# Projection on raw x with the row norm applied afterwards, and work moved around the first projection of a two-block kernel

## The reference

```python
hn = rmsnorm(h, mix_norm_pre)              # x * rsqrt(mean(x*x) + EPS) * g
proj = hn @ w_in                           # (256, 2048) @ (2048, 3616)
z, xbc, dt_raw, u = jnp.split(proj, split_at, axis=-1)
xbc = jax.nn.silu(dwconv_centred(xbc, conv_w, conv_b))     # 5 taps along the rows
dt = jax.nn.softplus(dt_raw + dt_bias)
y = y_fwd + y_bwd + xs * d_skip            # two chunked SSD scans, 16 heads, chunks of 128
y = y * jax.nn.silu(z)
y = y * lax.rsqrt(jnp.mean(y * y, axis=-1) + EPS) * norm_w  # over 512 channels
y_pool = pool_mixer(u, pool_w, pool_scale)                 # mean windows 2, 4, 8, 16
mix = jnp.concatenate([y_ssd, y_pool], axis=-1) @ w_out
h = h + rmsnorm(mix, mix_norm_post)
```

## Time and profile before

| | us |
|---|---|
| median of 3 runs | 2986.96 (2986.94 to 2986.97) |
| the profiled execution, its own time | 2987.04 |
| its span in the trace | 2985.3 |
| PE busy | 2897.9 (97%) |
| DVE busy | 1975.4 (66%) |
| ACT busy | 1346.4 (45%) |
| POOL busy | 15.8 |
| mean granted TensorE clock | 0.986 of full |

### The profile page before, as it was taken

The page is one execution under the profiler, slowest core; times in us unless marked ns, Lnnn a source line. Parts: engine busy times, 40 slices in busy tenths (PEclk is TensorE's granted clock), DMA queues, the critical chain, the costliest instruction groups (busy, mean ns, idle before and its releaser), DMA issues.

```text
span 2985.3 us, 34913 instructions
## 1 busy us (share of the span) xinstructions
PE 2897.9 (97%) x13750; PEld 2394.7 (80%) x13750; DVE 1975.4 (66%) x2531; ACT 1346.4 (45%) x1657; POOL 15.8 (1%) x33
## 2 busy tenths in 40 slices
PE   6998999999999999999999999999989999999999
PEld 6987878888888887778888777778878888888887
DVE  3765789898986666852437777767766656655444
ACT  3444454444444445632324555554444444444333
POOL 1000000000000000000000000000000000000000
PEclk8999999999999999999999999999999999999999
DMA  5443768778778777623346655547766777776564
GB/s 177 142 121 106 222 194 255 246 241 251 253 254 256 246 246 247 223 78 93 93 120 189 176 177 179 181 130 241 236 196 205 219 222 218 221 214 209 191 191 154
DMA packets 301692, 583.25 MB, mean 195 GB/s; under 512 B 20699, under 2 KB 21177, under 8 KB 300889
## 3 DMA queue, kind: packets, MB, share of 16 engines
q1 hardware_dynamic: 299705, 573.57, 62.1%
q0 software_dynamic: 1824, 7.46, 0.8%
HBM read 578.85 MB, written 2.10 MB: 195 GB/s over the span
## 4 chain that ended last, share of the span: by engine, by line
PE 92%; DVE 4%; ACT 1%; issue 1%; DMA 0%; SPq 0%; ACTq 0%; DVEq 0%
PE psum L496 21%; PE psum L499 21%; PE psum L498 21%; PE psum L554 3%; PE psum L556 3%; PE psum L555 3%; PE psum L2547 2%; PE psum L2549 2%; PE psum L2548 2%; PE psum L469 2%; PE psum L471 2%; PE psum L472 2%; PE psum L2565 1%; PE psum L2575 1%; PE psum L515 1%
## 5 line engine op out<-in xcount | busy, mean ns | idle before, releaser
L674 DVE TENSOR_TENSOR w_lo<-w_raw,w_hi 128x1024 fp32r<-128x1024 f32 x720 | 877.6, 1224 | 592.6 <-ACT w_hi L609 588.9
L609 ACT ACTIVATE w_hi<-w_raw 128x1024 fp32r<-128x1024 f32 x720 | 762.8, 1060 | 1048.4 <-PE psum L499 1046.2
L496 PE MATMUL psum<-w_hi,x_split 128*128 128x512 f32 x1984 | 782.9, 395 | 8.6 <-issue 5.3
L499 PE MATMUL psum<-w_hi,x_split 128*128 128x512 f32 x1984 | 775.0, 391 | 0.0
L498 PE MATMUL psum<-w_lo,x_split 128*128 128x512 f32 x1984 | 774.5, 390 | 0.0
L496 PEld LDWEIGHTS psum<-w_hi,x_split 128*128 128x128 f32 x1984 | 373.9, 188 | 86.1 <-issue 8.0
L499 PEld LDWEIGHTS psum<-w_hi,x_split 128*128 128x128 f32 x1984 | 373.6, 188 | 78.7
L498 PEld LDWEIGHTS psum<-w_lo,x_split 128*128 128x128 f32 x1984 | 374.2, 189 | 75.1
L654 DVE TENSOR_TENSOR w_lo<-w_raw,w_hi 128x1024 fp32r<-128x1024 f32 x104 | 126.8, 1225 | 238.6 <-ACT w_hi L591 238.6
L496 PE MATMUL psum<-w_hi,hidden_split 128*128 128x512 f32 x704 | 274.8, 390 | 0.0
L630 DVE SCALAR_TENSOR_TENSOR stat<-w_raw,conditions,stat 128x512 f32<-128x512 f32 x360 | 269.8, 750 | 6.8
(11 more groups left out here) (324 smaller groups left out, 3470.5 us busy)
## 6 DMA issues: line engine op xcount, KB each, us to landing
w_raw<-in_w_in SPq DMA_DIRECT2D x216, 512.0 KB, 3.7
w_raw<-in_w_ada SPq DMA_DIRECT2D x192, 512.0 KB, 4.6
w_raw<-in_w_ffn_up SPq DMA_DIRECT2D x176, 512.0 KB, 4.6
w_raw<-in_w_ffn_down SPq DMA_DIRECT2D x88, 512.0 KB, 5.6
w_raw<-in_w_ff_gate SPq DMA_DIRECT2D x88, 512.0 KB, 3.9
w_raw<-in_w_ff_up SPq DMA_DIRECT2D x88, 512.0 KB, 4.4
w_raw<-in_w_ff_down SPq DMA_DIRECT2D x88, 512.0 KB, 4.4
w_raw<-in_w_out SPq DMA_DIRECT2D x64, 512.0 KB, 5.1
```

The source lines that it names most:

```text
L496: nc.tensor.matmul(to, x_hi[:, tokens], hi, start=u == 0 and t == 0, stop=False, skip_group_check=True)
L499: mm = nc.tensor.matmul(to, x_lo[:, tokens], hi, start=False, stop=end and t == 1, skip_group_check=True)
L609: nc.scalar.activation(w_hi[:, b.slot(n)], raw[:, b.raw_slot(k)], ACT.Copy).then_inc(w_rounded, 1)
L674: nc.vector.tensor_tensor(w_lo[:, slot], raw[:, b.raw_slot(k)], r(w_hi[:, slot]), ALU.subtract).then_inc(w_split, 1)
```

## The change

- x is no longer scaled before it is turned. PE turns raw x, ACT and DVE split x times gain at once (`hi_pair`, `lo_pair`). The sums of squares move into the stream (ACT, steps 0 to 2). `r_spread` spreads 1/rms over the partitions as a row `RROW`, and DVE multiplies each group's PSUM by it: in place for B, C and xs, into the buffers for u and z, where ACT copied before. ACT applies silu to z from the buffer.
- SP loads the identity, one gain, then for each quarter of the columns two pieces of x and a weight block; all other parameters and the dt weights are loaded by POOL. Their turning on PE is behind unit 3.
- The dt product is made of split values (48 fp32r matmuls), channels of dt on the partitions, behind unit 4; two transposes follow at step 6.
- The running sums of dt are held as hi and lo (`ROWS`, 64 rows, fp32r), and `rows` uses them with a selector `SEL` (fp32r).
- The taps of a group are done 8 in its last step and 8 in the step behind it. `cumulate` is at step 11 (before 13), `dt_done` at 9 (before 10), `pool_product` at 48, 49, 50, 52.
- `y_stat` makes two columns instead of a spread row (8 matmuls with one column), the root and the reciprocal are of 128x2, and `y_spread` spreads the result. The second half of y (y products 30 and 31, `y_out(7)`, `gate_y(1)`, norm and split) is beside out's first group, and out's units wait for the mix splits in five pieces.
- `PAIR_AT`, the spacing of the SSD pairs by two steps from the second on, is the same in both kernels.

The diff, cut to its core:

```diff
+            sp.dma_start(C[:, 0:P], consts_d[:, 0:P]).then_inc(S("start_landed"), 16)
+            sp.dma_start(*params[0]).then_inc(S("start_landed"), 16)
+            for k in range(4):
+                for c in range(2):
+                    sp.dma_start(H[:, c, columns_of(k)], A["x"][0, c * P:(c + 1) * P, columns_of(k)]
+                                 ).then_inc(S(f"x_landed{k}"), 16)
+                sp.dma_start(raw[:, k], source("in", PHASES["in"].body[k])).then_inc(w_landed[k], 16)
...
+                    if name == "in" and k < 4:
+                        continue
+                    if name == "in" and k == RAW + 2:
+                        sp.dma_start(C[:, P:], consts_d[:, P:]).then_inc(S("consts_landed"), 16)
...
+            for to, src in params[1:]:
...
+            pool.dma_start(WDT, W_IN[:, :, 2560:2592]).then_inc(S("wdt_landed"), 16)
...
+        IN_TURN = [-1, -1, -1, -1, 0, 0, 1, 1]
...
-        POOL_AT = [49, 50, 52, 53]
+        POOL_AT = [48, 49, 50, 52]
+        MIX = [(8, 10), (10, 12), (12, 16), (0, 4), (4, 8)]
...
+            act.wait_ge(S("mix_gain"), 1)
+            for k in range(4):
+                hi_pair(act, "mix_pre", 2 * k, XS, lambda t: prm("mix_pre", t))
+                hi_pair(act, "mix_pre", 2 * k + 1, XS, lambda t: prm("mix_pre", t))
+                first_hi(k)
...
+            def x_square(c):
+                for k in range(4):
+                    act.wait_ge(S(f"x_landed{k}"), 32)
+                square_part(act, "mix_pre", H[:, c, :], c, 0, SQ0)
...
-                group_used(act, b, k)
                 if j < 3:
                     t0 = X_TILE[j]
+                    act.wait_ge(S("in_scaled"), j + 1)
                     first_tap(act, lambda f: accf(b.set(j), f), lambda f: XBC[:, t0 + f],
...
+            def z_silu(g):
+                act.wait_ge(evacuated, 2 + 6 + g)
+                nc.scalar.activation(SZ[:, 4 * g:4 * g + 4], SZ[:, 4 * g:4 * g + 4], ACT.Silu
+                                     ).then_inc(S("z_ready"), 1)
...
-                nc.scalar.activation(ST[0:32, :], PS[0:32, 6, :], ACT.Copy).then_inc(S("acum_rows"), 1)
+                nc.scalar.activation(ROWS[0:64], PS[0:64, 6, :], ACT.Copy).then_inc(S("acum_hi"), 1)
...
+            def in_early(n):
+                if n == IN_END - 1:
+                    group_used(act, PHASES["in"], n)
+                    mix_hi(0)
...
-                [(PRE_SPLIT[i], lambda k: kept_hi(act, "mix_pre", k, XS), i) for i in range(4, 8)] +
-                [(2, conditions, None), (5, dt_exp, None), (8, dt_ln, None), (14, acum_rows, None)] +
+                [(0, x_square, 0), (1, x_square, 1), (2, lambda _: std_act(act, "mix_pre"), None)] +
+                [(5, conditions, None), (7, dt_exp, None), (9, dt_ln, None), (12, acum_rows, None)] +
...
                 [(at + 1, pool_out, g) for g, at in enumerate(POOL_AT)] +
-                [(52, y_square, 0), (56, mix_hi, 2), (56, mix_hi, 3), (57, y_root, 0), (58, y_square, 1),
-                 (59, mix_hi, 0), (60, y_root, 1), (61, mix_hi, 1)], "in", IN_END)
-            stream_act(act, "in", in_evac, late)
+                [(49, y_square, 0), (54, y_root, 0), (56, mix_hi, 1), (56, mix_hi, 2), (57, mix_hi, 3), (57, z_silu, 1)],
...
+            for k in range(4):
+                lo_pair(dve, "mix_pre", 2 * k, XS, lambda t: prm("mix_pre", t))
+                lo_pair(dve, "mix_pre", 2 * k + 1, XS, lambda t: prm("mix_pre", t))
+                first_lo(k)
...
+            def skip_rows(_):
+                all_params(dve)
...
+            def params_copy(_):
+                dve.wait_ge(S("params_pe"), 1)
...
+            def dt_scale(_):
+                dve.wait_ge(S("dt_by_heads"), 1)
+                ch.wait()
+                nc.vector.tensor_tensor(ST[0:32, 0:L], PS[0:32, 4, 0:L], RROW[0:32], ALU.mult).then_inc(S("dt_scaled"), 1)
...
-                for j in others:
+                for j in others if only is None else only:
...
+                    nc.vector.tensor_tensor(acc(b.set(j)), acc(b.set(j)), over_tiles, ALU.mult
+                                            ).then_inc(S("in_scaled"), 1)
+                    dve.wait_ge(S("in_scaled"), j + 1)
+                    conv_half(j, 0)
...
+                    t = slice(4 * (j - 3), 4 * (j - 3) + 4)
+                    dve.wait_ge(S("u_padded"), 1)
+                    nc.vector.tensor_tensor(UP[:, t, 8:8 + L], acc(b.set(j)), over_tiles, ALU.mult).then_inc(evacuated, 1)
...
+                    z_scale(0)
...
+            def conv_half(j, half):
+
+                b, t0 = PHASES["in"], X_TILE[j]
+                conv(lambda f: accf(b.set(j), f), lambda f: XBC[:, t0 + f], 5,
+                     lambda tap, f: prm("ssd_conv_w", 12 * tap + t0 + f), lambda f: 4 * j + f + 1, evacuated,
+                     (0, 1) if half == 0 else (3, 4))
...
+                for s in range(2):
+                    nc.vector.scalar_tensor_tensor(DA[:, :, s], c32(dtv), -1.0, over_chunks(SM[:, 64:96]),
+                                                   ALU.mult, ALU.mult).then_inc(S("da_ready"), 1)
...
-                [(at, next_split, 4 + 2 * at) for at in range(2)] +
-                [(1, lambda_sums, None), (3, minus_lambda, None), (4, dt_bias, None), (6, dt_plus_one, None),
-                 (10, dt_done, None), (13, masked_cb, 0),
-                 (14, masked_cb, 1), (14, acum_columns, None)] +
+                [(8 * j + 8, lambda j: conv_half(j, 1), j) for j in range(3)] +
+                [(2, skip_rows, None), (3, params_copy, None), (3, lambda _: rstd_dve(dve, "mix_pre"), None),
+                 (3, wdt_lo, None), (4, rstd_row, None), (5, dt_scale, None), (5, lambda_sums, None), (6, dt_bias, None),
+                 (6, minus_lambda, None), (8, dt_plus_one, None), (9, dt_done, None), (12, acum_columns, None),
+                 (12, acum_lo, None), (13, masked_cb, 0), (14, masked_cb, 1)] +
...
-                [(STEP_AT[4 * t + 3] + 6, y_out, t) for t in range(8)] +
+                [(STEP_AT[4 * t + 3] + 6, y_out, t) for t in range(7)] +
...
-                [(51, gate_y, 0), (57, mix_lo, (0, 2)), (58, gate_y, 1), (58, mix_lo, (1, 3)), (59, y_recip, 0),
-                 (59, y_norm, 0), (60, mix_lo, (2, 0)), (61, y_recip, 1), (61, y_norm, 1), (62, mix_lo, (3, 1))],
...
+                [(48, gate_y, 0), (54, y_recip, 0), (56, mix_lo, 1), (56, y_norm, 0), (56, z_scale, 1), (56, mix_lo, 2),
+                 (57, mix_lo, 3)], "in", IN_END)
+            stream_dve(dve, "in", in_evac, late, early=lambda n: mix_lo(0) if n == IN_END - 1 else None)
...
+            def out_late(j, u):
+                if (j, u) == (0, 0):
+                    y_out(7)
+                    gate_y(1)
+                if (j, u) == (0, 2):
+                    y_recip(1)
+                if (j, u) == (0, 3):
+                    y_norm(1)
+                if (j, u) == (0, 4):
+                    mix_lo(4)
+
...
+            def r_spread(_):
+                k = RMS.index("mix_pre")
+                pe.wait_ge(rms_rstd, rms_count("mix_pre"))
+                pe.wait_ge(pre_ready, pre_count("mix_pre", 8))
+                for c in range(2):
+                    mm = nc.tensor.matmul(PS[:, 7, c * P:c * P + P], RS[:, k, c:c + 1].to_broadcast([P, P]), ident,
+                                          start=c == 0, stop=True, skip_group_check=True)
+                mm.then_inc(S("r_spread"), 1)
...
-                pe.wait_ge(pre_z, z_count("mix_pre", 8))
+                pe.wait_ge(S("wdt_split"), 1)
+                for t in range(KT):
+                    nc.tensor.matmul(PS[0:32, 4, 0:L], WDT_HI[:, t], XS[:, t, 0], start=t == 0, stop=False,
+                                     skip_group_check=True)
+                    nc.tensor.matmul(PS[0:32, 4, 0:L], WDT_HI[:, t], XS[:, t, 1], start=False, stop=False,
+                                     skip_group_check=True)
+                    mm = nc.tensor.matmul(PS[0:32, 4, 0:L], WDT_LO[:, t], XS[:, t, 0], start=False, stop=t == KT - 1,
...
-                pe.wait_ge(S("da_ready"), 1)
+                da = SM[:, 128:256].rearrange("p (c s h) -> p c s h", c=2, s=2)
...
+                    mm = nc.tensor.matmul(PS[:, 4 + m % 2, d * L:d * L + L], SEL[0:64, h:h + 1].to_broadcast([64, P]),
+                                          ROWS[0:64, d * L:d * L + L], start=d == 0, stop=True, skip_group_check=True)
...
+                pe.wait_ge(S("exponent_ready"), 15 + g)
                 pe.wait_ge(S("y_sq"), g + 1)
-                for t in range(4 * g, 4 * g + 4):
-                    mm = nc.tensor.matmul(PS[:, 2 + g, 0:L], const("ones"), YSQ[:, t], start=t % 4 == 0,
-                                          stop=t % 4 == 3, skip_group_check=True)
+                for c in range(2):
+                    for t in range(4 * g, 4 * g + 4):
+                        mm = nc.tensor.matmul(PS[:, 4 + g, c:c + 1], YSQ[:, t, c * P:c * P + P], const("ones")[:, 0:1],
```

(31 more changed lines are left out.)

249 lines of the change are left out of this document (121 added, 128 removed).

## The result

The changed kernel takes 2966.84 us, median of 4 runs (2966.21 to 2968.05); the kernel before, on the same chip, 2986.95 (2985.95 to 2986.97). The ratio is 0.9934, with a 95% interval of 0.9922 to 0.9947, so it is faster by 20.1 us, 0.7%. Forecast were 2960 (26.7 us less) and a range of 2948 to 2975. The profiled execution is that of 2966.21, with a span of 2964.4.

The account below looks back on a forecast made before the run. PE, busy 97% of the span, was taken to bound the kernel through its work, waits and half clock. From 2987.04 us, -22.2 + 7.0 - 0.9 - 9.2 + 0.8 - 2.2 = -26.7 gave 2960.3, stated as 2960; range 2948 to 2975.

Parts of the forecast that it names:

- The start: Up to unit 5: PE turns raw x as quarters land, unit 0 at 11.1 instead of 31.5; -22.2 us.
- DVE's evacuation: First groups, DVE multiplying PSUM by 1/rms before the taps: cumulate waits 5.4 us, plus clock loss; +7.0 us.
- The 1.6 for the clock: At cumulate: idle time also costs PE clock, a third of ten us at half; some 1.6 us lost.
- Steps 15 to 27: Phase "in" after the first groups: DVE-chain waits stay and eat four pairs' cheaper rows; the whole stretch gives 0.9 us.
- The rows: Row matmuls per pair, fp32r with 64 rows instead of fp32 with 32: 0.77 us less, 12 pairs counted; -9.2 us.
- The +0.5 for z and u by DVE: Steps 31 and 39: DVE products replace ACT's copies ahead of the mix matrix; +0.5 us with the pooling windows.
- The end: Out's first group: y work beside its units, PE waits of 2.7 and 2.9 us, twice 1.6 at half clock; -2.2 us.
- From 320 us on: The rest of the kernel, untouched by the change: a difference over 1 us would show the prediction wrong.
- rival 1: Step 11: DVE has more room than counted, cumulate hardly waits, 7.0 falls away; 2953 us, chance 0.12.
- Rival 2: Head start handed back: waits behind unit 3, dt product at half clock, longer waits at 11 and 19; 2972, chance 0.15.
- rival 3: SSD pairs: the row matmul is no cheaper, or DVE's pair chain binds instead; 2969 us, chance 0.06.
- Rival 4: Early units: PE, fed by loops that stop it, stays at 1.2 GHz; 3007 over units 0 to 20, chance 0.05.

Follow-up runs that it names:

- The variant with no wait at either place: The changed kernel with the B, C product and cumulate both behind unit 13, and their DVE and ACT followers moved: 2960.89 us.
- the second pair: The changed kernel and the kernel before, unedited, each run and profiled once more: 2966.49 and 2986.09 us.
- the first pair: The original profiled executions of the kernel before and the changed kernel: medians 2986.95 and 2966.84 us.
- three reorderings around the new waits: The changed kernel with dt product behind unit 5, B, C product and cumulate behind unit 13, out's first-group chains moved up: 2944.85 us.

## Why the prediction was right, and where not

*What bounds the kernel.* That PE's waits and half clock decide, and DVE's order sets the waits, held in the main. Of the waits named in the text, those behind unit 3, at cumulate, the two of 120 to 135 us and the two at the end stand in the trace within 0.7 us of their forecast. The one at the row spread is not there.

*The start, -22.2; measured -23.7 and -22.9.* Unit 0 came 1.3 later than said, since the first turn of x began at 5.91 and the later one waited 2.06 at 9.94 for the second quarter. From there the number is better than its working. The wait behind unit 3 was 3.1 instead of 3.7, and DVE was done with the dt weights at 36.4 instead of 38.1, so PE did not wait at the spread. But unit 4, forecast at full clock, took 4.34 us instead of 2.88 behind that wait, and no term was set down for this. The misses cancel in part, and unit 5 was 1.5 earlier than said. The bound of -24.7 with unit 0 at full clock is -24.4 by the prediction's own 5.1 and 2.88.

*DVE's evacuation, +7.0; measured +8.2 and +9.5 from unit 8 to unit 16.* The wait of 5.4 was right (5.26), in part by luck. With T the end of unit 7 (51.55), the first eight taps began at T+5.3 and not T+4.7, and so dt_plus_one ended at T+12.9 and not T+12.3. ACT's table load for dt_ln, 1.28 us in the forecast's chain, was not in it: it stood at 59.81, in idle time, and ACT then waited 3.37 for DVE. What held dt_done until T+13.9 was a w_lo ahead of it, which the forecast's chain doesn't have. The 1.6 for the clock was the mis-sized step. It took the share of a stretch of ten us that held a wait of 1.9; behind a wait of 5.3 all of cumulate ran at half (4.57 against 2.3), and unit 12 with the B, C product took 0.6 longer than before in one execution and 1.9 in the other, so 2.9 to 4.2. The variant with no wait at either place wins 8.2 from unit 8 to unit 14.

*Steps 15 to 27, -0.9; measured -0.8 and +2.1.* The waits of 1.92 and 1.35 stayed, and the chains behind silu and mix_matrix came where the forecast had put them, as two new waits of 1.27 and 2.23. The agreement of -0.8 is chance in part: the second pair has one half-clock stretch more after and one fewer before, and that isn't the change's.

*The rows, -9.2.* Right mechanism, size off. A pair gives 0.63, not 0.77. The 11 pairs from unit 28 on give -6.9 where -8.4 was forecast; the twelfth, in step 27, keeps its gain too (unit 27 to 28 takes 4.30 at full clock in the run with 32 rows, against 4.90 before), but lies under a half-clock stretch in both executions of the changed kernel. The +0.5 for z and u by DVE doesn't show. The run with fp32 rows shows that the term is the row matmuls, and the one with 32 rows that the number of rows doesn't count. The bound of -10.2 is -9.8 by the prediction's own 1.06 and two times 0.12.

*The end, -2.2; measured -0.3 and -0.6, once the sums of squares in phase "in" (1.8) are counted with it.* Both waits were right, and each was charged 1.6 for the clock. The second cost that (unit 6 took 4.45 instead of 2.72). The first cost twice as much: 1.6 in the small matmuls and 1.7 in unit 3 (4.47). The bound of +1 with each wait doubled is too low: 2.7 and 2.9 more give +3.4.

*From 320 us on, 0; measured +2.2 and -0.5.* The prediction named a difference of over 1 us as a sign that it is wrong, and it would have been one by the first pair. It was too strict: the same program differs from itself by 2.4 us there.

*The rivals.* The wait of 5.26 at cumulate excludes rival 1. Rival 2 had a part of the truth, as what was missing came from half clock behind waits, but the dt product did not fall to half in either execution (5.5 us for 48 matmuls), and the head start was not handed back there. The fp32 run excludes rival 3. Rival 4 saw the danger of feeding PE by loops, and its size was wrong: over 0 to 80 us the granted clock was 0.94, some 10 us at half, and unit 0 at the pace of half clock comes on top.

*The Trainium skill's drain* in "What ACT_TABLE_LOAD costs" of "ScalarE: Activation LUTs" would have added 1.4 us to each table load. In the changed kernel the load at 65.68 takes 1.28 and its activation starts at 66.97, 0.01 behind its end, so the trace again shows none. And of the two chains that the prediction would have lengthened by it, the second would not have grown by 1.4: that load stood in idle time of ACT.

## What to carry to other kernels

Price a new wait on the bound engine by what runs behind it as well: here the half clock behind waits of 2.7 to 5.3 us cost 1.5 to 4.2 us a wait where it came, in one case more than the wait itself (3.3 behind 2.9). When a wait names the link of a chain, moving the waiting instruction alone buys a part of it, here about half, as the next link stands there; move the chain's followers on every engine at once, and check what stands behind an in-order w_lo that itself waits. And an edit that starts PE 19 us earlier is not finished when it works: three reorderings around the new waits took another 22 us.

## What the runs showed of the hardware

- The granted clock differs between executions of one program. A stretch at 1.2 GHz followed the same wait of 1.92 us in one execution and not in the other (0.72 against 1.00 over 110 to 116 us), for 1.3 to 1.5 us each. The Trainium skill's "TensorE: Matmul & The Clock Gate", section "What's actually happening", says of a kernel's first matmuls that the point at which the clock rises varies from run to run; here a fall and rise vary in the middle of one as well.
- A stretch at half clock behind a wait of 3.1 to 3.3 us cost about 1.5 us in whatever work stood there: 3.08 us behind unit 3 and unit 4 took 4.34 instead of 2.88; 3.28 us in front of the row spread and the 48 matmuls of the dt product took 7.06 instead of 5.54. It doesn't always come: in the run with all taps in one piece the same wait of 3.08 left the clock at 1.00 over 32 to 37 us, where the changed kernel has 0.66.
- A pair of fp32r matmuls of 256 columns with switched weights takes 0.43 us with 32 rows as with 64, and the pair of fp32 ones with 32 rows 1.06.
- Loading 256 KB quarters of x and blocks of 512 KB in turn, SP issued each block in 0.43 to 0.53 us (the last one stands below, in SP's timeline of the changed kernel); the 1.07 that the forecast took from the earlier trace rows (6.40 for six, issued in a row behind x and the parameters) does not carry over. Why those took longer is not shown.

```profile
7.63 0.53 SPq L976 DMA_DIRECT2D w_raw<-in_w_in  x1
```
